# Merge stage of a hybrid decoder layer: weights loaded ahead of a wait, weight splits in two parts, two window products on ScalarE, and early loads for the second half

## The reference, cut to what matters

```
weights = jax.nn.softmax(jnp.stack(lses, axis=0), axis=0)
out = jnp.sum(weights[..., None] * jnp.stack(outs, axis=0), axis=0)
...
y_attn = attention_branch(q, k, v) * jax.nn.silu(g_attn)
...
merged = (gates[:, :, 0] * (y_ssm @ p_ssm)
          + gates[:, :, 1] * (y_attn @ p_attn)
          + gates[:, :, 2] * (y_sc @ p_sc))
out = merged @ w_out
```

## Time and profile before

| | |
|---|---|
| Timed runs | 2956.4, 2965.29, 2966.23 us (median 2965.29) |
| Profiled execution: time | 2955.61 us |
| Profiled execution: span | 2954.0 us |
| PE busy in the span | 2819.0 us (95%) |
| DVE, ACT, POOL busy | 1591.4, 1207.5, 1581.1 us |
| Merge stage: first to last matmul | 2333.4 to 2752.2 us |

### The profile page before, as it was taken

How to read it: one execution, slowest core, us unless ns; L and a number is a source line. 1 busy time by engine, 2 the same in 40 slices (tenths; PEclk the granted TensorE clock), 3 DMA queues, 4 the chain that set the end, 5 groups by cost and what they waited for, 6 DMA issues and landing times. The chain is left out here.

```text
span 2954.0 us, 40344 instructions
## 1 busy us (share of the span) xinstructions
PE 2819.0 (95%) x14222; PEld 2377.4 (80%) x14222; DVE 1591.4 (54%) x2540; ACT 1207.5 (41%) x2099; POOL 1581.1 (54%) x1064
## 2 busy tenths in 40 slices
PE   6999999999999999999989999998999788999798
PEld 5888888888877888888878888888999766778687
DVE  6335234996524457865335555555667585733333
ACT  5332234332225443332325555555666533332332
POOL 7778778777768787777754445442111253222000
PEclk8999999999999999999999999998999899999999
DMA  4648346432225364322354546456555467953543
GB/s 121 161 145 246 114 124 157 118 115 79 72 93 192 110 170 128 108 86 72 90 174 136 178 145 185 139 162 211 165 155 158 152 196 236 301 156 114 185 149 107
DMA packets 462800, 436.04 MB, mean 148 GB/s; under 512 B 60736, under 2 KB 403008, under 8 KB 454976
## 3 DMA queue, kind: packets, MB, share of 16 engines
q1 hardware_dynamic: 457472, 415.30, 47.5%
q10 hardware_dynamic: 2880, 10.49, 1.0%
q0 software_dynamic: 2304, 8.39, 0.7%
HBM read 290.99 MB, written 143.13 MB: 147 GB/s over the span
## 5 line engine op out<-in xcount | busy, mean ns | idle before, releaser
L531 PE MATMUL p_acc<-h_kept,w_hi 128*128 128x512 f32 x1216 | 477.4, 393 | 5.0 <-ACT work L577 3.1
L533 PE MATMUL p_acc<-h_kept,w_lo 128*128 128x512 f32 x1216 | 475.5, 391 | 0.0
L532 PE MATMUL p_acc<-h_kept,w_hi 128*128 128x512 f32 x1216 | 474.1, 390 | 0.0
L417 POOL TENSOR_TENSOR w_lo<-p_sums,w_hi 128x512 fp32r<-128x512 f32 x300 | 391.4, 1322 | 135.1 <-ACT w_hi L618 135.1
L618 ACT ACTIVATE w_hi<-p_sums 128x512 fp32r<-128x512 f32 x300 | 189.3, 632 | 477.0 <-PE p_acc L533 451.1
L531 PEld LDWEIGHTS p_acc<-h_kept,w_hi 128*128 128x128 f32 x1216 | 228.7, 188 | 54.5 <-ACT work L577 3.3
L533 PEld LDWEIGHTS p_acc<-h_kept,w_lo 128*128 128x128 f32 x1216 | 228.8, 188 | 49.7
L532 PEld LDWEIGHTS p_acc<-h_kept,w_hi 128*128 128x128 f32 x1216 | 228.9, 188 | 48.7
L531 PE MATMUL p_acc<-p_ops,w_hi 128*128 128x512 f32 x608 | 241.2, 397 | 7.1 <-DVE p_ops L719 7.1
L533 PE MATMUL p_acc<-p_ops,w_lo 128*128 128x512 f32 x608 | 239.0, 393 | 0.0
L532 PE MATMUL p_acc<-p_ops,w_hi 128*128 128x512 f32 x608 | 237.2, 390 | 0.0
(11 more groups left out here) (322 smaller groups left out, 6713.8 us busy)
## 6 DMA issues: line engine op xcount, KB each, us to landing
raw<-w_in SPq DMA_DIRECT2D x100, 512.0 KB, 5.2
p_rawb<-w_in SPq DMA_DIRECT2D x76, 512.0 KB, 5.2
s_qs<-p_stage SPq DMA_DIRECT2D x96, 256.0 KB, 4.0
work<-s_gates SPq DMA_DIRECT2D x48, 512.0 KB, 7.2
s_xbc<-p_stage SPq DMA_DIRECT2D x32, 512.0 KB, 2.6
work<-s_xbc SPq DMA_DIRECT2D x16, 1024.0 KB, 7.0
spare<-s_qs SPq DMA_DIRECT2D x16, 1024.0 KB, 5.4
att_all<-s_att SPq DMA_DIRECT2D x24, 528.0 KB, 5.6
```

Of the source, the lines that this page charges most:

```text
L417: tt(w_lo[:, k], weight(u, k), w_hi[:, k], ALU.subtract).then_inc(w_made, 1)
L531: pe.matmul(bank, hi, ops[k][:, 0, c], start=c == 0, stop=False)
L532: pe.matmul(bank, hi, ops[k][:, 1, c], start=False, stop=False)
L533: last = pe.matmul(bank, lo, ops[k][:, 0, c], start=False, stop=c == 3)
```

## The change

- SP issues the first load of weights (unit 1's) at the start of the stage, ahead of the wait for the attention stores.
- ACT's and POOL's splits of a unit's weights are in two instructions each: the first eight chunks (p_ssm), then the rest. PE's lane 0 waits for the first part only (`w_first_made`), the other lanes for all (`w_made`). Loads of the two parts have semaphores of their own. Unit 8's p_ssm is loaded one unit earlier, during unit 4.
- In unit 0 ACT splits y_sc ahead of unit 1's weights, and DVE takes the low part of chunk 11 from POOL.
- `load_att` loads patterns 0 and 2 when the sums of the pair before are made, and pattern 1 when that pair has been transposed.
- ACT weighs two of the six products (patterns 1 and 2 of the second 128 tokens), as 16 activations of 128x64 with a scale per partition; DVE keeps three. DVE's sums wait for ACT's share (`share_made`).
- Second half: chunks 0 to 2 of y_ssm are loaded by SP into the attention's buffer behind the last transposes; ACT loads chunks 3 to 7, waits for the three, splits them, then loads y_sc and splits chunks 3 to 7. DVE makes six low parts, not two, ahead of unit 11's last lane.

```diff
-    NM, UNITS, LATE, FULL, SECOND, LAST = DM // P, 20, 4, 8, 12, 11
+    NM, UNITS, LATE, FULL, SECOND, AHEAD, SSM_N = DM // P, 20, 4, 8, 12, 3, 8
+        y_ahead = [att_all[:, c * HALF:(c + 1) * HALF] for c in range(AHEAD)]
...
@@ SP
                 def load_att(pair):
-                    sp.wait_ge(turned, pair + 1)
-                    for g in range(3):
+                    if pair:
+                        sp.wait_ge(o_made, pair)
+                        sp.wait_ge(o1_made, pair)
+                    for g in (0, 2, 1):
+                        if g == 1:
+                            sp.wait_ge(turned, pair + 1)
...
+                load_weights(0, 1)
                 for g, stores in enumerate((1, PATTERNS[1][1], 1)):
                     sp.wait_ge(att_stored[g], 16 * stores * (SLOTS // 2 + 1))
                 load_att(0)
...
-                    if u == 0:
-                        load_weights(0, 1)
...
-                    ahead = {LATE - 2: range(LATE, FULL), LATE - 1: (), LATE: (), LATE + 1: (FULL,), LATE + 2: ()}
+                    ahead = {LATE - 2: range(LATE, FULL), LATE - 1: (), LATE: (), LATE + 1: (), LATE + 2: ()}
+                    if u in (LATE, LATE + 1):
+                        load_weights(FULL, FULL, (0,) if u == LATE else (1, 2))
...
+                    elif u == SECOND - 1:
+                        sp.wait_ge(turned, pair + 2)
+                        for c in range(AHEAD):
+                            sp.dma_start(y_ahead[c], d["y_ssm"][c, :, HALF:]).then_inc(ahead_loaded, 16)
@@ POOL
                 def split(u, k, at):
+                    if at.start == 0:
+                        first = slice(0, SSM_N)
+                        pool.wait_ge(w_first_hi, whole_unit(u) + 1 if isinstance(u, int) else u - 3)
+                        tt(w_lo[:, k, first], raw[:, first], w_hi[:, k, first].bitcast(F32), ALU.subtract
+                           ).then_inc(w_first_made, 1)
+                        at = slice(SSM_N, at.stop)
                     pool.wait_ge(w_hi_made, u + 1)
...
-                    if u == 0:
-                        pool.wait_ge(y_hi_made, LAST + 1)
-                        tt(y_lo[LAST], y_raw[LAST], y_hi[LAST].bitcast(F32), ALU.subtract).then_inc(y0_last, 1)
@@ ACT
-                    copy(w_hi[:, k, at], raw_of(u if at.start else 0, at)).then_inc(w_hi_made, 1)
+                    if at.start == 0:
+                        first = slice(0, SSM_N)
+                        copy(w_hi[:, k, first], raw[:, first]).then_inc(w_first_hi, 1)
+                        act.wait_ge(raw_loaded[1], raw_at[1])
+                        at = slice(SSM_N, at.stop)
+                    copy(w_hi[:, k, at], raw_of(u if at.start == 12 else 0, at)).then_inc(w_hi_made, 1)
...
                     act.activation(ex[:], low[:], ACT.Exp, scale=-1.0).then_inc(ex_made, 1)
+                    act.wait_ge(ex_scaled, pair + 1)
+                    for g in (1, 2):
+                        for a in range(SLOTS // 2):
+                            for h in range(2):
+                                part = att[:, 1, g, a, h * OUT_W:h * OUT_W + HDIM]
+                                last = act.activation(part, part, ACT.Copy, scale=ex[:, 1, g, 2 * a + h:2 * a + h + 1])
+                    last.then_inc(share_made, 1)
...
                 for u in range(SECOND):
-                    split(u + 1, (u + 1) % 2, chunks_of(u + 1), raw_count(u + 1))
                     if u == 0:
                         hi_of_y(1, 0)
+                    split(u + 1, (u + 1) % 2, chunks_of(u + 1), [raw_count(u + 1, part) for part in range(2)])
...
-                load_y(0, 1)
+                load_y(0, 1, range(AHEAD, SSM_N))
+                act.wait_ge(ahead_loaded, 16 * AHEAD)
+                for c in range(AHEAD):
+                    copy(y_hi[c], y_ahead[c]).then_inc(y_hi_made, 1)
                 act.wait_ge(acc_made[1], SECOND - 2)
                 load_y(1, 1)
-                hi_of_y(0, 1)
+                for c in range(AHEAD, SSM_N):
+                    act.wait_ge(y_loaded[c // 4], 16 * (SSM_N - AHEAD - 4) if c < 4 else 64)
+                    copy(y_hi[c], y_raw[c]).then_inc(y_hi_made, 1)
@@ PE
-                    pe.wait_ge(w_made, u + 1)
+                    if first != LATE:
+                        pe.wait_ge(w_first_made, u + 1 if first < LATE else u - 3)
                     for lane, br in lanes(first, k):
                         _, _, at, n = BRANCHES[br]
+                        if at:
+                            pe.wait_ge(w_made, u + 1)
@@ DVE
-                        for g in range(2 + t):
+                        for g in range(2 - t):
                             last = tt(halves(t, g), halves(t, g), share(t, g), ALU.mult)
                         last.then_inc(part_made, 1)
                     window = lambda g: halves(1, g)
                     dve.wait_ge(part_made, 2 * pair + 2)
+                    dve.wait_ge(share_made, pair + 1)
...
-                        lo_of_y(range(FIRST_Y, LAST), 0, y0_made)
+                        lo_of_y(range(FIRST_Y, 12), 0, y0_made)
...
-                        lo_of_y(range(2), 12, y1_made)
+                        lo_of_y(range(6), 12, y1_made)
```

More of the change, by code:

```diff
@@ L1801, in lanes, with raw_count, whole_unit @@
             return [(0, 0), (1, 1)] if u < LATE else [(k, 2)] if u < FULL else [(0, 0), (1, 1), (2, 2)]
-        def raw_count(u):
-            return 32 * u if u < LATE else 48 * u - 240
+        def raw_count(u, part):
+            return 16 * u if u < LATE else 16 * (u - 4) if part == 0 else 32 * u - 176
+        def whole_unit(u):
+            return u if u < LATE else u - 4
         with nc.Block() as block:
@@ L1944, in _, with load_y @@
                 act.sem_inc(y_stored, 16)
+                act.sem_inc(w_first_hi, 1)
                 copy = lambda to, of: act.activation(to, of, ACT.Copy)
-                def load_y(br, half):
+                def load_y(br, half, chunks=None):
                     y, _, first, n = BRANCHES[br]
-                    for c in range(n):
+                    for c in chunks or range(n):
                         act.dma_start(y_raw[first + c], d[y][c, :, half * HALF:(half + 1) * HALF]
@@ L1962, in split @@
                         act.wait_ge(late_loaded[u - LATE], 16)
-                    elif raw_at is not None:
-                        act.wait_ge(raw_loaded, raw_at)
+                    else:
+                        act.wait_ge(raw_loaded[0], raw_at[0])
                     v = u - 2
@@ L2006, in _ @@
                         u = SECOND + 2 * i + k
-                        split(u + 1, 1 - k, chunks_of(SECOND), 48 * u - 192)
+                        split(u + 1, 1 - k, chunks_of(SECOND), [16 * u - 48, 32 * u - 144])
                         gates(u, lanes(SECOND, k))
-                split(UNITS - 1, 1, chunks_of(SECOND), raw_count(UNITS - 1))
+                split(UNITS - 1, 1, chunks_of(SECOND), [raw_count(UNITS - 1, part) for part in range(2)])
                 for u in range(UNITS - 2, UNITS):
@@ L2027, in products @@
                                 pe.wait_ge(ya_made, 2 * t + 3)
-                            if first == 0 and c == LAST:
-                                pe.wait_ge(y0_last, 1)
-                            elif first in (0, SECOND) and t == 0:
+                            if first in (0, SECOND) and t == 0:
                                 pe.wait_ge(y1_made if first else y0_made, c + 1)
@@ L2124, in lo_of_y @@
                         dve.wait_ge(y_hi_made, base + c + 1)
-                        tt(y_lo[c], y_raw[c], y_hi[c].bitcast(F32), ALU.subtract).then_inc(made, 1)
+                        tt(y_lo[c], y_ahead[c] if base and c < AHEAD else y_raw[c], y_hi[c].bitcast(F32), ALU.subtract
+                           ).then_inc(made, 1)
                 for u in range(SECOND):
```

20 lines of the change are left out of this document (12 added, 8 removed).

## The result

The changed kernel takes 2940.8 us (median of 4 runs, 2938.8 to 2945.7) against 2962.4 us (4 runs, 2956.4 to 2966.2): a ratio of 0.9936 with a 95% interval of 0.9911 to 0.9961. A second set of runs gave 2941.4 us (10 runs) against 2958.1 us (13 runs), ratio 0.9953 (0.9939 to 0.9967). The change makes the kernel 0.5 to 0.6% faster; 2943 was predicted, and a gain of 17.6 us.

What follows compares the result with a forecast made beforehand. PE's gaps in the merge stage were taken as all that could be won: 6.0 + 2.6 + 6.2 + 1.0 + 1.8 = 17.6 us. From a base of 2960.5 us this gave 2943 us, range 2927 to 2957.

Steps and rivals of the forecast that it cites:

- What bounds the stage: Merge stage: matmuls at full clock cannot be improved, their number stays, so all that can be won lies in PE's gaps.
- Unit 0: Start of merge stage: y split first, down at 2348.6; unit 0's transposes start 5.9 us earlier, say 6 (3 to 10).
- The mixing: Eight merging units: two products moved to ACT gain 0.8 us each (0 to 2.1), as POOL's last sum blocks DVE's first.
- Units 1 to 3: Earlier attention loads and split weights gain 0.95 and 1.7 us in units 1 and 2; unit 3's transposes stay PE-bound.
- Unit 8: The 7.49 us gap ahead of it goes; its transposes, hanging on unit 9's weights through ACT, gain 6.2 us (3 to 8).
- T(9) to T(11): Transpose starts of units 9 to 11: three gaps of 0.43 us, with shorter mixing off the path, gain 1.0 us.
- Second half: From unit 12: early y chunks land 12 us after unit 11's transposes start; unit 13 gains 1.8 us (slow bound: loss 1.2).
- The sign that I had named for being wrong here: Second half: PE's first matmul of unit 12 later than 17 us after unit 11's transposes start would show the forecast wrong.
- The floor that I gave it by the gates: Second half, fast landing at 9 us: gain 3.3 us, held by gates that now wait for DVE's six chunks.
- Rival 3: Second half: kernel slower because ACT's wait for SP's three early chunks delays y_sc and y_attn, deciding from landing near 29.6 us; chance 0.05.
- The sum: Whole merge stage: 6.0 + 2.6 + 6.2 + 1.0 + 1.8 = 17.6 us, the profiled execution to 2938.0 us.
- The base: Whole kernel: starting time for the forecast of runs, put at 2960.5 us, midway between profiled execution and the runs' median.

## Why the prediction was right, step by step

**What bounds the stage.** Right: all that was won lay in PE's gaps; behind unit 13 the interval to the output stage is the same in all profiles within 0.5 us.

**Unit 0.** The mechanism was right, the size a little low: T(0) gained 7.6 and 8.2 us for a forecast of 6. y was down at M+14.1 where I had 15.2; and T(0) came 0.6 us sooner after it than I had counted. The weights beside y cost it 0.6 to 1.4 us where I took 2.5, within the bounds of 0 and 3. What I did not see is that the early load, the first edit in the change's own list, adds nothing to the order on ACT: either alone brings T(0) to M+30.3 to 31.3, both together to M+30.9 and 31.7.

**The mixing.** DVE's blocked first sum was forecast to end at +6.1 from the first product and the second at +6.8; measured +5.76 and +6.49, a gain of 1.07 for a forecast of 0.8 and a naive 2.1. An activation cost 0.245 us (3.93 / 16), forecast 0.24. (I had read the stretched product of the earlier trace rows as ending with POOL's; by its own figures it ends 0.55 us behind, as the first sum does here.) The step that was too small is where it counts: I gave it units 0, 1, 2 and 8 and 0.4 us in three loops; the run without it is later by 5 to 6.5 us at T(11), since the loops to T(10) and T(11) then take 23.3 us instead of 22.7, and the longer gap ahead of T(2) can cost unit 3 its clock.

**Units 1 to 3.** Forecast 2.6 us together, measured 1.6 in the first pair of profiles and 3.3 in the second; the 1.6 us between them are unit 3's half clock in the kernel before. The cause I named for it, the attention loads in two steps, is refuted: with ACT's share taken out T(0) to T(3) are 59.0 us, beside 57.8 and 59.4 in the kernel before, so the shorter mixing did it. What split weights add was not run by itself.

**Unit 8.** Forecast 6.2 us at T(8), and that the 7.49 us gap would move to ahead of the transposes at about 7 us. Measured: T(3) to T(8) 50.9 and 50.0 us against 57.5 and 57.0, so 6.1 to 7.5; gap 5.21. Scaled weights came 6.6 us ahead of T(8), forecast 6.9. The run with the mixing first shows that T(8) hung on the weight splits; the run without the early load shows that unit 9's weights follow POOL's end on unit 8, as forecast.

**T(9) to T(11).** Forecast 1.0 us; measured 70.2 and 70.7 us against 72.3 and 71.6: 0.9 to 2.1.

**Second half.** Here the sum was wrong in its sign. I took the chunks as landed at T(11)+12 and had +15 as the slow end, with a loss of 1.2 us; they came at T(11)+14.9. After 10.86 us of idle time the clock stayed at half for 13 matmuls, 5.7 us where they take 3.0 at full clock: 2.7 us lost, not 1.6 (1.3 in the second profile). Instead of a gain of 1.8 us there is a loss of 0.9 to 2.4. The sign that I had named for being wrong here, unit 12's first matmul past T(11)+17, came: it was at T(11)+17.4 in both profiles. The mis-sized term is the landing: 4.7 MB at 402 GB/s. The rate was right. These rows are from T(11) to T(11)+13.1, and on to where ACT goes on:

```profile
2548.37:2561.45 13.08, 6.50 (x33) 5.20 (x31) 4.08 (x4) 1.00 (x2) 0.00 (x0) 0.87 1.05 391
2561.45:2563.28 1.83, 0.00 (x0) 0.00 (x0) 0.00 (x0) 0.00 (x1) 0.00 (x0) 0.50 0.19 76
```

13.08 us at 391 GB/s and 1.83 at 76 are 5.25 MB. The 0.5 MB more than I had counted must have been issued earlier; the last load of unit 13's weights went out 3 us ahead of T(11), and these loads took 8 to 10 us to land. That it is they is an estimate; no run shows it apart. The rest is the last 1.8 us, in which almost nothing moves any more and ACT still waits; I had no term for it. The floor that I gave it by the gates did not bind. Rival 3, that ACT's wait for SP's chunks decides, was the right place with a price of 2 us, far from the 17 it needed.

**The sum.** 17.6 forecast, 15.8 to 18.4 by the marks: unit 0 gave 2 us more, unit 8 up to 1, and the second half 3 to 4 less. That the sum fits so well is partly luck, since these errors have opposite signs. The base midway between the profiled execution and the median was close: the kernel before measured 2962.4 and 2958.1. Against the profiled execution alone the forecast of 2938.0 fits less well (2945.7), 5.9 us of it from M.

## What to carry to other kernels

When a gap closes, look at once for what the same engine will wait for next: an early load that let PE start a unit 2.7 us sooner gave 1 to 2 us at its transposes, since they hung on an Exp queued behind the weights of the unit after. An in-order engine that serves two chains should do the one with the tighter date first; moving one pair of steps past each other in one unit was worth 7 us, nearly as much as the largest part of the change. And a load issued from another queue isn't early if a wait for it stands ahead of your own issues.

## What the runs showed of the hardware

**The same code ahead of the stage takes 2330 to 2347 us.** One place repeats in two forms: PE waits 1.6 us for DVE near 929 us in eight of the fourteen profiles (1.5 in one of them) and 4.3 us in the other six, the first profile of the changed kernel among them. In all six the clock falls behind it (0.66 to 0.92 in the stretch below, 1.00 in the other eight). In the first profile of the changed kernel 26 matmuls run in 8 us where 37 do in the kernel before:

```profile
925.00:933.00 8.00, 8.00 (x26) 4.99 (x25) 1.26 (x2) 0.63 (x1) 6.62 (x6) 0.70 0.00 0
933.00:941.00 8.00, 8.00 (x36) 5.17 (x35) 0.00 (x0) 0.85 (x2) 4.03 (x4) 1.00 0.53 131
```

```profile
925.00:933.00 8.00, 8.00 (x37) 4.29 (x35) 0.05 (x1) 0.00 (x0) 7.92 (x7) 1.00 0.23 61
```

(the first fence after, the second before). It can't explain the scatter of M: the eight profiles with the short wait hold both the earliest M (2330) and the two latest (2345 and 2347), those with the long one lie between 2336 and 2342. What moves M stays open.

**The shared reads of DVE and POOL** show in every row here: operations of 16 columns on DVE took 0.16 us alone and up to 2.36 beside POOL, where they ended with POOL's operation. The Trainium skill, SBUF — State Buffer, Who interferes with whom, has this as an exclusive lock between a DVE operation with two SBUF inputs and a GpSimd operation that reads SBUF; the rows agree. The sixteen activations on ACT beside both took 3.93 us with POOL and DVE busy, 0.245 us each, near the 0.24 that I had worked out from the earlier trace rows.

**A short queue beside a long one.** The slowest of SP's three chunks took 11 us from issue beside five loads of ACT's, and 15.9 and 16.9 in the two kernels where nine stood beside them.

**The half clock behind a gap.** Behind the same gap ahead of unit 12 (10.3 to 11.0 us in eight profiles) PE ran 6 to 13 matmuls at 1.2 GHz, one each 0.43 us, before it was back at one each 0.23 us: 1.3 to 2.7 us lost. The two profiles of the changed kernel hold both ends of this.
